# Experts' weight steps in pairs: gate and up of two blocks as 512 moving columns, down rows two steps later

## The reference

```python
(jax.nn.silu(xb @ w_gate[e]) * (xb @ w_up[e])) @ w_down[e]
```

## Time and profile before

| what | value |
|---|---|
| median of 3 runs | 2253.8 us (2251.62 to 2254.12) |
| profiled execution | 2254.85 us, of which the span is 2252.7 |
| mean granted clock of TensorE | 0.976 of full speed |
| experts, first gather piece to last down product | about 1790 to 2237.5 us |
| TensorE, VectorE, ScalarE busy over the span | 94%, 68%, 48% |
| read from HBM | 397.71 MB |

### The profile page before, as it was taken

One profiled execution on the slowest core, in us unless ns is written; L12 is line 12 of the kernel. 1 busy time (PEld: TensorE's weight loads), 2 busy tenths in 40 slices (PEclk: granted clock), 3 DMA queues, 4 the chain that ended last, 5 costly groups with the idle time before them and its releaser, 6 DMA issues.

```text
span 2252.7 us, 37570 instructions
## 1 busy us (share of the span) xinstructions
PE 2123.5 (94%) x14715; PEld 1953.6 (87%) x14715; DVE 1527.7 (68%) x2103; ACT 1080.4 (48%) x1589; POOL 453.9 (20%) x205
## 2 busy tenths in 40 slices
PE   7999988999999997999998998999987799999997
PEld 7999977999999995899896788999976699999996
DVE  5566886666665656665668456666675488888887
ACT  4434533433543444544443124334444477777775
POOL 2223222222222230222221232222320000000000
PEclk9999999999999999999998999999988799999999
DMA  8555411555555540555531004555441289888885
GB/s 324 195 179 173 161 57 58 186 195 178 172 185 194 177 168 29 173 184 194 187 141 57 1 1 159 190 180 190 151 167 39 94 282 323 312 317 316 312 316 196
DMA packets 73267, 400.62 MB, mean 178 GB/s; under 512 B 8240, under 2 KB 8368, under 8 KB 41136
## 3 DMA queue, kind: packets, MB, share of 16 engines
q1 hardware_dynamic: 72704, 397.22, 51.0%
q10 hardware_dynamic: 432, 1.57, 0.2%
HBM read 397.71 MB, written 1.05 MB: 177 GB/s over the span
## 4 chain that ended last, share of the span: by engine, by line
PE 83%; DVE 9%; ACT 3%; issue 2%; PEld 1%; POOL 1%; DMA 0%; DVEq 0%; SPq 0%; ACTq 0%; PEldq 0%
PE psum L302 24%; PE psum L303 24%; PE psum L304 23%; DVE w_lo L286 2%; PE psum L899 2%; PE psum L889 1%; PE psum L2340 1%; PE psum L312 1%; ACT w_hi L279 1%; POOL w_lo L292 1%; PE psum L2353 1%; DVE r_e L2052 1%; PE psum L880 1%; PE psum L1637 0%; PE psum L2382 0%
## 5 line engine op out<-in xcount | busy, mean ns | idle before, releaser
L286 DVE TENSOR_TENSOR w_lo<-ring,w_hi 128x1024 fp32r<-128x1024 f32 x496 | 768.6, 1576 | 309.7 <-ACT w_hi L279 308.8
L279 ACT ACTIVATE w_hi<-ring 128x1024 fp32r<-128x1024 f32 x744 | 742.1, 1051 | 354.0 <-PE psum L304 207.4
L292 POOL TENSOR_TENSOR w_lo<-ring,w_hi 128x1024 fp32r<-128x1024 f32 x160 | 402.7, 2517 | 1148.7 <-ACT w_hi L279 1148.7
L302 PE MATMUL psum<-fT_hi,w_hi 128*128 128x256 f32 x1760 | 500.3, 284 | 10.0 <-DVE w_lo L286 9.8
L303 PE MATMUL psum<-fT_lo,w_hi 128*128 128x256 f32 x1760 | 499.0, 284 | 0.0
L304 PE MATMUL psum<-fT_hi,w_lo 128*128 128x256 f32 x1760 | 499.0, 283 | 0.0
L302 PE MATMUL psum<-w_hi,hT_hi 128*128 128x256 f32 (+3 forms) x1216 | 379.6, 312 | 16.2 <-issue 7.9
L303 PE MATMUL psum<-w_lo,hT_hi 128*128 128x256 f32 (+3 forms) x1216 | 367.1, 302 | 0.0
L304 PE MATMUL psum<-w_hi,hT_lo 128*128 128x256 f32 (+3 forms) x1216 | 366.9, 302 | 0.0
L302 PEld LDWEIGHTS psum<-fT_hi,w_hi 128*128 128x128 f32 x1760 | 338.4, 192 | 17.0 <-issue 6.9
L303 PEld LDWEIGHTS psum<-fT_lo,w_hi 128*128 128x128 f32 x1760 | 338.5, 192 | 3.7
(11 more groups left out here) (461 smaller groups left out, 2580.8 us busy)
## 6 DMA issues: line engine op xcount, KB each, us to landing
ring<-in_stream SPq DMA_DIRECT2D x248, 1024.0 KB, 5.0
ring<-in_stream SPq DMA_DIRECT2D x248, 512.0 KB, 4.2
tables<-in_tables SPq DMA_DIRECT2D x1, 2453.0 KB, 19.9
gain_row<-in_gains ACTq DMA_DIRECT2D x3, 512.0 KB, 3.7
rows<-in_rows SPq DMA_DIRECT2D x1, 1288.0 KB, 24.2
X<-in_x SPq DMA_DIRECT2D x1, 1024.0 KB, 4.9
result<-X SPq DMA_DIRECT2D x2, 512.0 KB, 2.7
columns<-in_columns SPq DMA_DIRECT2D x1, 993.0 KB, 14.9
```

Source lines behind the costliest of these rows:

```text
L279: act.activation(part(w_hi, g, i), ring[:, k, i * PART:(i + 1) * PART], ACT.Copy) \
L286: dve.tensor_tensor(part(w_lo, g, i), ring[:, k, i * PART:(i + 1) * PART], part(w_hi, g, i).bitcast(F32), ALU.subtract) \
L292: pool.tensor_tensor(part(w_lo, g, 2), ring[:, k, 2 * PART:STEP], part(w_hi, g, 2).bitcast(F32), ALU.subtract) \
L302: pe.matmul(out_, w[0], x[0], start=first, stop=False, skip_group_check=True)
```

## The change

1. Blocks are taken in pairs (`unit`): (0, 1), ..., (8, 9), and block 10 alone. The gate columns of both, then the up columns of both, stand side by side in the stream (`expert_steps`), so a matmul moves 512 columns. The first step of a pair holds 4 of the 8 slices of features, the second the other 4: 12 matmuls of 512 columns a step, where 24 of 256 were. A pair fills one bank. Block 10 has its 24 of 256.
2. `silu`, `gated`, `act_hi` and `act_lo` are done once per pair, on 256 columns. The two transposes of a pair come behind the first quarter of the next pair's slices.
3. Down rows stand two steps later in the stream (`DOWN_LAG`): step g multiplies block g - 2. Steps 0 and 1 have none (the loads still bring their late parts), and one step more at the end holds the rows of the last two blocks in its early part. Rounding of down rows comes one step earlier than before against the step in which they stand.
4. An expert's result is taken in step 1 of the next in place of step 0, with `act_hi` and `act_lo` right behind it; the additions come in steps 2 (two), 3 and 4 in place of 1 to 4.
5. `act_lo` stands before the step's pick, additions and pieces on VectorE, where it stood behind them.
6. The late part of a step is loaded right behind its early part, where the early part of the next step came between.

The branch for two tiles changes likewise and does not run here. The diff, without the other branch's helpers:

```diff
-STEPS = {"ffn": FF_STEPS, "moe": EXPERTS * EXPERT_STEPS, "final": 0, "delta": DELTA_T + DELTA_K + OUT_STEPS,
+STEPS = {"ffn": FF_STEPS, "moe": EXPERTS * EXPERT_STEPS + 1, "final": 0, "delta": DELTA_T + DELTA_K + OUT_STEPS,
...
-        UP_BANK, AUX_BANK = 4, 6
+        UP_BANK, AUX_BANK, DOWN_LAG = 4, 6, 2
         CHUNKS = [(t, h) for t in range(TT) for h in range(2)]
...
-            out_ = [(e - 1, "result", 0)] if s == 0 and e > 0 else []
+            out_ = [(e - 1, "result", 0)] if s == 1 and e > 0 else []
             out_ += [(e + 1, "pick", 0)] if s == 1 and not last else []
-            out_ += [(e - 1, "chunk", s - 1)] if 1 <= s <= len(CHUNKS) and e > 0 else []
+            out_ += [(e - 1, "chunk", c) for c in {2: (0, 1), 3: (2,), 4: (3,)}.get(s, ()) if e > 0]
...
+        def unit(m):
+
+            e, s = divmod(m, EXPERT_STEPS)
+            first = m - s % 2
+            return -(-EXPERT_STEPS // 2) * e + s // 2, [f for f in (first, first + 1) if f < EXPERT_STEPS * (e + 1)]
+
+        def up_bank(u, j, tiles):
+
+            return psum[:, UP_BANK + (j if tiles == 2 else u % 2), :]
+
+        def up_products(u, n, tiles, o):
+
+            banks = psum[:, UP_BANK:UP_BANK + 2, :] if tiles == 2 else psum[:, UP_BANK + u % 2:UP_BANK + u % 2 + 1, :]
+            return banks[:, :, o * n * P:(o + 1) * n * P]
...
-            def up(m, halves):
+            def up(m, after_quarter=None):
 
                 e, s = divmod(m, EXPERT_STEPS)
...
+                (u, fs), g = unit(m), moe_first + m
+                width_ = 2 * P * len(fs)
+                per_step = KT // len(fs)
+                if s == 0:
+                    pe.wait_ge(even_taken, half * e + half)
+                    pe.wait_ge(odd_taken, half * e + half)
+                pe.wait_ge(lo_ready, 2 * g + 2)
+                if m == fs[0]:
+                    pe.wait_ge(ffn_act_ready, f0 + u - (0 if tiles == 2 else 1))
+                for i in range(per_step):
+                    k = (s % 2) * per_step + i if len(fs) == 2 else i
+                    for j in range(tiles):
+                        rows_ = [gathered(x, tiles, e % 2, k)[:, j * P:(j + 1) * P] for x in (hT_hi, hT_lo)]
+                        ins = three_passes(pe, up_bank(u, j, tiles)[:, 0:width_], rows_,
+                                           [x[:, g % 2, i * width_:(i + 1) * width_] for x in (w_hi, w_lo)], k == 0, k == KT - 1)
+                    if after_quarter is not None and i == per_step // 4 - 1:
+                        after_quarter()
+                ins.then_inc(ffn_up_ready, 1)
+
+            def turn(m):
+
+                u, fs = unit(m)
+                pe.wait_ge(ffn_gated, 2 * (f0 + u) + 1)
+                for i, f in enumerate(fs):
+                    for j in range(tiles):
+                        ins = pe.transpose(up_bank(u, 0, tiles)[:, (f % 2) * SEQ + j * P:(f % 2) * SEQ + (j + 1) * P],
+                                           by_tile(gated, u, len(fs), tiles)[:, j, i * P:(i + 1) * P], ident)
                 ins.then_inc(turned_ready, 1)
 
-            def down(m):
-
-                f, g = f0 + m, moe_first + m
-                pe.wait_ge(lo_last_ready, g + 1)
-                pe.wait_ge(ffn_act_ready, f + 1)
+            def down(f, g, part_):
+
+                e, s = divmod(f, EXPERT_STEPS)
+                pe.wait_ge(ffn_act_ready, f0 + unit(f)[0] + 1)
                 if s == 0 and e > 0:
                     pe.wait_ge(y_ready, 2 * tiles * e)
                 for j in range(tiles):
                     for h in range(2):
-                        c = slice(2 * D_MODEL + h * 512, 2 * D_MODEL + (h + 1) * 512)
+                        c = slice(part_ * PART + h * 512, part_ * PART + (h + 1) * 512)
                         ins = three_passes(pe, psum[:, 2 * j + h, :], [x[:, f % 2, j * P:(j + 1) * P] for x in (act_hi, act_lo)],
                                            [x[:, g % 2, c] for x in (w_hi, w_lo)], s == 0, s == EXPERT_STEPS - 1)
                 ins.then_inc(steps_used, 1)
...
             for p in range(n_pieces):
                 piece(0, p, True)
             for m in range(MOE_STEPS):
-                up(m, (0,))
-                if m > 0:
-                    turn(f0 + m - 1)
-                up(m, (1,))
-                if m > 0:
-                    down(m - 1)
+                fs = unit(m)[1]
+                up(m, (lambda: turn(m - 1)) if tiles == 1 and m == fs[0] and m > 0 else None)
+                if m < DOWN_LAG:
+                    pe.nop().then_inc(steps_used, 1)
+                else:
+                    pe.wait_ge(lo_last_ready, moe_first + m + 1)
+                    down(m - DOWN_LAG, moe_first + m, 2)
                 pe.wait_ge(ffn_up_ready, f0 + m + 1)
                 pe.nop().then_inc(early_used, 1)
...
-            turn(f0 + MOE_STEPS - 1)
-            down(MOE_STEPS - 1)
+            pe.wait_ge(lo_ready, 2 * total)
+            down(MOE_STEPS - 2, total - 1, 0)
+            if tiles == 1:
+                turn(MOE_STEPS - 1)
+            down(MOE_STEPS - 1, total - 1, 1)
...
-            split_hi(act, moe_first, moe_first)
+            split_hi(act, moe_first, moe_first, (0, 1))
             split_hi(act, moe_first + 1, moe_first + 1, (0, 1))
+            for g in range(moe_first, moe_first + DOWN_LAG):
+                k, n = in_ring(g, g)
+                act.wait_ge(late_loaded[k], 16 * n)
+            act.nop().then_inc(hi_last_ready, DOWN_LAG)
...
+            def round_act(m):
+
+                u, fs = unit(m)
+                act.wait_ge(turned_ready, u + 1)
+                act.wait_ge(steps_used, moe_first + m + 1)
+                act.activation(act_of(act_hi, fs, tiles), turned_unit(u, fs, tiles), ACT.Copy).then_inc(ffn_gated, 1)
+
+            def result(e, parity):
+
+                act.wait_ge(steps_used, moe_first + EXPERT_STEPS * (e + 1) + DOWN_LAG)
...
-                f, g = f0 + m, moe_first + m
-                act.wait_ge(ffn_up_ready, f + 1)
-                act.wait_ge(ffn_act_ready, f - 1)
-                act.activation(by_tile(silu, f, tiles), up_products(f, tiles)[:, :, 0, :], ACT.Silu).then_inc(ffn_silu_ready, 1)
+                (u, fs), g = unit(m), moe_first + m
+                if m == fs[-1]:
+                    act.wait_ge(ffn_up_ready, f0 + m + 1)
+                    act.wait_ge(ffn_act_ready, f0 + u - (0 if tiles == 2 else 1))
+                    act.activation(by_tile(silu, u, len(fs), tiles), up_products(u, len(fs), tiles, 0), ACT.Silu).then_inc(ffn_silu_ready, 1)
                 if g + 2 < total:
                     split_hi(act, g + 2, g + 2, (0,))
                 for x, what, p in jobs(m, tiles):
                     if what == "result":
-                        result(x, x % 2, g - 1)
+                        result(x, x % 2)
+                        round_act(m)
                 if g + 2 < total:
                     split_hi(act, g + 2, g + 2, (1,))
                 for x, what, p in jobs(m, tiles):
                     if what == "piece" and p % 2 == 0:
                         piece(x, x % 2, p)
-                act.wait_ge(turned_ready, m + 1)
-                act.wait_ge(steps_used, g - 1)
-                act.activation(act_hi[:, f % 2, 0:slots], psum[:, UP_BANK + f % 2, 0:slots], ACT.Copy).then_inc(ffn_gated, 1)
-                if g + 1 < total:
-                    split_hi(act, g + 1, g + 1, (2,))
-            result(EXPERTS - 1, (EXPERTS - 1) % 2, total - 1)
+                if m == fs[-1] and not result_in(m, tiles):
+                    round_act(m)
+                if g + 2 < total - 1:
+                    split_hi(act, g + 2, g + 2, (2,))
+            result(EXPERTS - 1, (EXPERTS - 1) % 2)
...
+            def rounded(m):
+
+                u, fs = unit(m)
+                dve.wait_ge(ffn_gated, 2 * (f0 + u) + 2)
+                dve.tensor_tensor(act_of(act_lo, fs, tiles), turned_unit(u, fs, tiles), act_of(act_hi, fs, tiles).bitcast(F32), ALU.subtract) \
+                   .then_inc(ffn_act_ready, 1)
...
-                f, g = f0 + m, moe_first + m
-                dve.wait_ge(ffn_silu_ready, f + 1)
-                dve.tensor_tensor(by_tile(gated, f, tiles), by_tile(silu, f, tiles), up_products(f, tiles)[:, :, 1, :], ALU.mult) \
-                   .then_inc(ffn_gated, 1)
-                split_lo_last(dve, g, g)
+                (u, fs), g = unit(m), moe_first + m
+                if m == fs[-1]:
+                    dve.wait_ge(ffn_silu_ready, f0 + u + 1)
+                    dve.tensor_tensor(by_tile(gated, u, len(fs), tiles), by_tile(silu, u, len(fs), tiles), up_products(u, len(fs), tiles, 1),
+                                      ALU.mult).then_inc(ffn_gated, 1)
+                if moe_first + DOWN_LAG <= g + 1 < total - 1:
+                    split_lo_last(dve, g + 1, g + 1)
                 for x, what, p in jobs(m, tiles):
                     if what == "result":
                         result(x, x % 2)
```

(43 more changed lines are left out.)

38 lines of the change are left out of this document (15 added, 23 removed).

## The result

The changed kernel takes 2237.84 us in the median of 4 runs (2236.75 to 2240.69), the kernel before 2253.61 beside it: 0.9935 of its time, 95% interval 0.9923 to 0.9947. It was timed twice more, on other chips: 2240.82 against 2252.62 (0.9940, 0.9925 to 0.9955) and 2239.28 against 2253.18 (0.9942, 0.9928 to 0.9956). So it is 12 to 16 us faster, about 13.5. A gain of 8.6 us was forecast, with the time inside 2239 to 2252. The direction held; the size did not.

The account below looks back on a forecast made before the run. TensorE was taken to bound the kernel, with 0.80 us lost once per expert. 2254.85 - 6.2 - 3.2 + 0.8 = 2246.2 us, less 1.05 for the median of the runs, gave 2245.2 us, range 2239 to 2252.

Parts of the forecast that it names:

- Term 1: Gate and up products in the experts: 960 matmuls of 512 columns, each 0.0065 us cheaper than two of 256, 6.2 us less.
- my lower bound of 0.2258: Time in us of a 512-column gate or up matmul if each further column cost only its 1/2.4 ns.
- the bound of 11.9: Most that wider gate and up products could save, in us, at 0.2258 us per 512-column matmul.
- The Trainium skill's rule: Matmuls start N / 2.4 + 2.5 ns apart, so wider products save 2.4 us; as a rival 2249.0 us, chance 0.04.
- Term 2: Transposes moved to two in a row per pair: same number, 88, at 0.11 us each, so nothing.
- Term 3: Each pair's chain from product to `act_lo`: ready with 0.7 us of cover, so all hidden.
- Term 4: Boundary of two experts: 0.80 us gap gone, 0.35 us left at a later wait, seven times, 3.2 us less.
- Term 5: First steps, without down products as cover: about 0.5 us of wait plus 0.3 at step 3, 0.8 us more.
- Term 6: Loads: one more step of 1 MB, 3.3 us of transfer, hidden; landings at most 8.1 us against 8.4 of cover.
- the one that wins more: Rival: wide products near 0.2258 us and no boundary wait, 2237.1 us, chance 0.07.
- The slower ones: Rivals: each pair waiting for `act_lo`, 2265 us, chance 0.11; 1.2 us lost at seven expert boundaries, 2251.1 us, chance 0.08.

Follow-up runs that it names:

- narrow version: Changed kernel with each 512-column gate and up matmul made as two of 256 again, all else kept: 2251.34 us, 0.9991 of the kernel before.

## Why the prediction was wrong

*Term 1, the wider products*, is the step that failed: the mechanism held, the size did not. I took 0.2317 us for a wide matmul from the down products before, "the same tile sizes and types with another weight tile". They were the nearest rows, but six in a row behind narrow ones each time, so all of them show the slow beginning of a run. In a long run a wide one takes 0.2267, which is my lower bound of 0.2258 nearly, and the 66 down products of an expert, which I counted at nothing, gained 0.25 us with it. 6.2 us were forecast; width is worth 9.4 by the sums per expert (8.5 in gate and up, 2.0 in the down products, less 1.0 by the longer wait behind the additions), 8.7 in the stretch from mark to norm and 10.5 in the medians. Gate and up do not reach the bound of 11.9, because transposes and gather pieces break their runs: there a wide one gains 1.06 / 120 us, or 8.8 ns, where settled ones would gain 12.

The Trainium skill's rule ("TensorE: Matmul & The Clock Gate", the fixed cost per matmul), N / 2.4 + 2.5 ns, gave 2.4 us for this term, about a quarter of what width is worth. The trace agrees with it at neither width: the settled 226.7 ns are nearer to its 215.8 than 231.7 were, the narrow one stays at 119 to 120 against 109.2.

*Term 2, transposes*: nothing, right; gate, up and transposes of the narrow version take 33.26 us per expert, as before without its gap.

*Term 3, the pair's chain*: right. `act_lo` was waited for in the first pair only, and as before in the last block.

*Term 4, the boundary*: the 0.80 gone and 0.34 left, at the `w_lo` of step 3, as worked out, though at six boundaries. But 3.2 us were too few: the narrow version, which differs from the kernel before by all but width, wins 0.73 us per expert, 5.1 over seven. What I left out is the second delay of 0.14 us one step later, and that the first matmul behind a wait is itself 0.07 to 0.11 us slower. I also left out that VectorE's load there, not the place of one instruction, sets the wait: in the kernel before, the same move alone lost time.

*Term 5, the start*: 0.8 us forecast, counted for two waits for `w_lo`. TensorE's idle time was 0.34 us for `w_lo`, 0.69 for `gated` and 0.20 for `act_lo`, and from start to start 1.9 us were lost. The table load that came onto the path was the thing overlooked, about 1.0 us of it; I had read the ScalarE rows there from 1805.09 on, and the load stood at 1797.71. From the mark to the second `m_back` both kernels take 52.9 us in the mean, so the first expert keeps nothing of what the wider products win in it.

*Term 6, the loads*: hidden, right, but not by the cover that I gave: landings took up to 9.3 us against 8.4 of cover, and in one profile of three ScalarE waited for them.

So 9.4 + 5.1 - 1.9 are 12.6 us, and the stretch shows 12.7. That the two agree so well is in part luck, since the stretch scatters by 2 us and the last boundary and the end were not counted by themselves. Against the forecast of 8.6, width brought about 3 us more, the boundary 1.9 more, and the start took 1.1 more. Of the rivals, the one that wins more named the right pitch and, with 2237.1 us, nearly the measured time; but it counted 11.9 us for width and no boundary wait at all, so its number is met by luck as well. I gave it 0.07. The slower ones did not come: no pair waited, and the boundary got better.

## What to carry to other kernels

A pitch is a property of a sequence, not of an instruction: before taking a duration from "the same form elsewhere", look at what stands ahead of it there, and whether the change makes its runs longer. A wait costs more than its idle time, since the first matmuls behind it are slow too: count from start to start. Where an engine behind the bound was full for several steps, moving one instruction moved the wait, twice; a new order of all of them won half, and work taken out of the full steps won the rest. And when the first activation of a kind moves, its table load moves along.

## What the runs showed of the hardware

- Matmuls of 128 x 128 weights and 512 fp32r columns at the full clock start 0.23 to 0.24 us apart at the head of a run and 0.2267 from the fifth to eleventh on; with 256 columns 0.119 to 0.120 us throughout. Behind a wait of TensorE the first of 512 columns takes 0.305 to 0.34 us. At half clock, at 1796 to 1799 us, 512 columns take 0.427 us and 256 columns 0.213, exactly twice, so that there width is worth nothing.
- The load of `silu`'s table takes 1.28 us on ScalarE, in each run.
- Two executions of one kernel differ by up to 6 us ahead of the experts, and their half-clock time by up to 17 us.
